# Two FFNs, an output projection and a pooling mixer joined into one stage over two token halves

## The chip, the cores and the metric

One of the eight cores of a Trainium2 chip runs the whole program. The metric is the device time of one execution in microseconds, the median of several executions. Besides the kernel there is nothing on the chip.

## What is computed

One inference step of a two-layer hybrid decoder, in fp32: 1024 prompt tokens and 8 sequences of 8 sample tokens, 1088 tokens of width 1024. Layer 0 mixes tokens by multi-head latent attention, layer 1 by causal mean pooling over windows of 2, 4, 8 and 16 tokens in four groups of 256 channels. Each mixer is followed by a gated FFN with a causal depthwise convolution of width 3. Around each sub-layer stand norms, with scale, shift and gate per sequence:

```python
xp = xp + g_mp[:, None, :] * rms_norm(op, norm_mix_post[i])
hp = modulate(xp, norm_ffn_pre[i], sh_fp, sc_fp)
...
u = h @ w_up                                   # 1024 -> 2 x 2816
up = jnp.concatenate([prev, u], axis=1)
conv = conv_b + up[:, 0:T] * conv_w[0]
for k in range(1, CONV_W):
    conv = conv + up[:, k:k + T] * conv_w[k]
y = (jax.nn.silu(conv[..., :D_FF]) * conv[..., D_FF:]) @ w_down
...
xp = xp + g_fp[:, None, :] * rms_norm(fp, norm_ffn_post[i])
```

Outputs are x of all tokens, the new attention cache rows, and the pooling and convolution states.

## The kernel before, in words

Channels lie on the partitions, tokens on the free axis; `k.x` holds x as 8 tiles of 128 channels by 1088 tokens. The tokens are cut into three chunks of 384, 384 and 320 columns (`CHUNKS`; the last has the 64 sample tokens). Precision comes from splitting each operand into a high part and a low part in fp32r, and each product is three matmuls: high by high, high by low, low by high. ScalarE makes the high part (`split_hi`, L1753), VectorE the low one (`split_lo`, L1814).

The stages follow one another, with a barrier between them (`stage_done`): `adaln_stage`, three attention stages, `mla_out_stage`, `ffn_stage(0)`, `pool_stage`, `ffn_stage(1)`.

- `mla_out_stage` multiplies the attention output by `wo` in 8 units of 128 rows (L1429 to L1431) and empties PSUM on ScalarE (L1390). Then comes `Exit`.
- `Exit` norms the result y: squares on ScalarE (L86), sums by a matmul with ones (L113), root (L95), turned to columns (L122), reciprocal on VectorE (L128), spread over the partitions (L143). VectorE multiplies y by gate and reciprocal (L519) and adds it to x (L524), half of the tiles on GpSimd (L532). It also takes the norm of the new x.
- `Entry` makes the next stage's input: x by scale and reciprocal (L418), shift and high part on ScalarE (L441), low part (L427, L431).
- `ffn_stage` runs over 22 pairs p: 128 gate channels G and 128 linear channels U each. Per pair SyncE fetches three units of 512 KB (L1720); TensorE forms G in three chunks of 8 x 3 matmuls, then U, and after each 3 matmuls of U one down product of the pair before (`down`, 3 matmuls into one of two banks, L1915 to L1917). ScalarE empties the banks (L1767, L1770), VectorE adds the other two taps (L1826, L1830), ScalarE does SiLU (L1794) and g's high part (L1789), VectorE the product (L1874) and g's low part (L1878). VectorE adds every down product to y in SBUF (`accumulate`, L1857), 24 per pair; `down` waits for `acc_done`, so that a bank is emptied before it is used again.
- `pool_stage` adds up window sums by doubling, two groups on VectorE (L1517, L1624) and two on GpSimd (L1517, L1556, L1557), those of the samples on VectorE (L1615, L1619), multiplies by four 256 x 256 matrices in plain fp32 (L1652, two passes each) and ends in `Exit`.

The order of the work on each engine is written out in the program: each engine has its own queue, in order, and semaphores tie them.

## Time and profile before

| | |
|---|---|
| median of 3 runs | 2976.69 us (2976.57 to 2980.84) |
| the profiled execution | 2976.89 us |
| its span, first to last instruction | 2975.1 us, 43092 instructions |
| mean granted clock of TensorE | 0.958 |
| TensorE busy | 2696.2 us (91%) |
| VectorE busy | 1772.6 us (60%) |
| ScalarE busy | 1028.8 us (35%) |
| GpSimd busy | 99.8 us (3%) |

The page cuts the span into 40 slices of 74 us, with the busy share in tenths (9 is 90% or more). The output projection begins at 959 us, FFN 0 at 1112, the pool mixer at 1970, FFN 1 at 2112. A granted clock of 1.00 is 2.4 GHz, 0.50 is 1.2 GHz.

### The profile page before, as it was taken

What the parts mean: (1) busy time and instruction counts of PE and PEld (TensorE: products, weight loads), DVE (VectorE), ACT (ScalarE), POOL (GpSimd) and SP (SyncE); (2) the same over time, 40 slices, a digit from 0 to 9 for tenths busy, and PEclk for the clock granted to TensorE, in tenths of its full rate; (3) what the DMA queues carried; (4) which work ended last, traced back from release to release, by engine and by line L of the source; (5) the groups of instructions that cost most, each with busy time, mean ns of one, the idle gap of its engine ahead of it and who ended that gap; (6) DMA issues with size and microseconds to landing.
All of it is one profiled execution on the core that took longest, in us unless ns stands there. A gap on an engine that the chain in (4) does not pass through costs nothing. (4 is left out here: it accounts for less than half of the span.)

```text
span 2975.1 us, 43092 instructions
## 1 busy us (share of the span) xinstructions
PE 2696.2 (91%) x15678; PEld 2321.5 (78%) x15678; DVE 1772.6 (60%) x3116; ACT 1028.8 (35%) x1692; POOL 99.8 (3%) x71
## 2 busy tenths in 40 slices
PE   6979699889978988999999999867799999999996
PEld 2558466666656958999999999723599999999993
DVE  3961355555623146666666666665666666666665
ACT  4842243434413144333333333233433333333322
POOL 0000000000000020000000000042100000000001
PEclk8989899999989999999999999988899999999998
DMA  7920100000063210111111111000111111111101
GB/s 295 413 75 32 48 12 22 11 25 0 1 209 107 103 36 29 43 43 51 50 47 42 42 42 42 13 29 0 43 47 51 50 43 42 42 42 42 42 28 66
DMA packets 42730, 178.48 MB, mean 60 GB/s; under 512 B 6146, under 2 KB 9730, under 8 KB 38690
## 3 DMA queue, kind: packets, MB, share of 16 engines
q1 hardware_dynamic: 41938, 176.81, 16.5%
q8 instruction: 45, 0.74, 0.1%
q10 hardware_dynamic: 720, 0.71, 0.1%
q14 instruction: 27, 0.22, 0.0%
HBM read 170.43 MB, written 7.07 MB: 60 GB/s over the span
## 5 line engine op out<-in xcount | busy, mean ns | idle before, releaser
L1857 DVE TENSOR_TENSOR ffn_y<-psum,ffn_y 128x384 f32<-128x384 f32 (+1 forms) x1056 | 554.7, 534 | 495.7 <-PE psum L1917 495.1
L1915 PE MATMUL psum<-ffn_h_hi,ffn_w_hi 128*128 128x384 f32 (+1 forms) x2112 | 692.9, 328 | 18.3 <-DVE ffn_h_lo L431 18.3
L1916 PE MATMUL psum<-ffn_h_lo,ffn_w_hi 128*128 128x384 f32 (+1 forms) x2112 | 695.4, 329 | 0.0
L1917 PE MATMUL psum<-ffn_h_hi,ffn_w_lo 128*128 128x384 f32 (+1 forms) x2112 | 692.1, 328 | 0.0
L1915 PEld LDWEIGHTS psum<-ffn_h_hi,ffn_w_hi 128*128 128x128 f32 x2112 | 399.1, 189 | 19.0 <-DVE ffn_h_lo L431 18.9
L1917 PEld LDWEIGHTS psum<-ffn_h_hi,ffn_w_lo 128*128 128x128 f32 x2112 | 399.4, 189 | 0.0
L1916 PEld LDWEIGHTS psum<-ffn_h_lo,ffn_w_hi 128*128 128x128 f32 x2112 | 399.0, 189 | 0.0
L1915 PE MATMUL psum<-ffn_g_hi,ffn_w_hi 128*128 128x384 f32 (+1 forms) x1056 | 357.6, 339 | 19.5 <-DVE ffn_g_lo L1878 15.1
L1916 PE MATMUL psum<-ffn_g_lo,ffn_w_hi 128*128 128x384 f32 (+1 forms) x1056 | 346.8, 328 | 0.0
L1917 PE MATMUL psum<-ffn_g_hi,ffn_w_lo 128*128 128x384 f32 (+1 forms) x1056 | 346.5, 328 | 0.0
L1767 ACT ACTIVATE ffn_u<-psum 128x384 f32<-128x384 f32 (+1 forms) x264 | 119.7, 454 | 548.4 <-PE psum L1917 442.8
L1915 PEld LDWEIGHTS psum<-ffn_g_hi,ffn_w_hi 128*128 128x128 f32 x1056 | 199.2, 189 | 52.9 <-DVE ffn_y L1857 28.7
L1826 DVE SCALAR_TENSOR_TENSOR ffn_work<-ffn_u,ffn_taps,ffn_work 128x1024 f32<-128x1024 f32 x176 | 225.4, 1281 | 16.0 <-ACT ffn_work L1770 13.5
L1916 PEld LDWEIGHTS psum<-ffn_g_lo,ffn_w_hi 128*128 128x128 f32 x1056 | 199.6, 189 | 0.0
L1917 PEld LDWEIGHTS psum<-ffn_g_hi,ffn_w_lo 128*128 128x128 f32 x1056 | 199.4, 189 | 0.0
L1770 ACT ACTIVATE ffn_work<-psum,ffn_taps 128x384 f32<-128x384 f32 (+1 forms) x264 | 172.9, 655 | 0.0
L1794 ACT ACTIVATE ffn_work<-ffn_work 128x1088 f32<-128x1088 f32 x44 | 49.0, 1114 | 351.1 <-DVE ffn_work L1830 351.1
L1814 DVE TENSOR_TENSOR ffn_w_lo<-ffn_raw,ffn_w_hi 128x1024 fp32r<-128x1024 f32 x132 | 157.5, 1219 | 20.6 <-ACT ffn_w_hi L1753 20.3
L1753 ACT ACTIVATE ffn_w_hi<-ffn_raw 128x1024 fp32r<-128x1024 f32 x132 | 135.6, 1065 | 49.5 <-DMA ffn_raw<-in_ffn_w 47.3
L1076 PE MATMUL psum<-keys,q 128*128 128x512 f32 (+3 forms) x384 | 146.2, 490 | 2.1 <-ACT prob L907 1.3
L914 ACT ACTIVATE prob_t<-psum 128x512 f32<-128x512 f32 (+3 forms) x128 | 66.2, 517 | 215.0 <-PE psum L1092 214.5
L337 DVE TENSOR_TENSOR ada_w_lo<-ada_w,ada_w_hi 128x2048 fp32r<-128x2048 f32 x48 | 107.7, 2287 | 23.1 <-ACT ada_w_hi L271 22.8
(230 smaller groups left out, 3637.1 us busy)
## 6 DMA issues: line engine op xcount, KB each, us to landing
ffn_raw<-in_ffn_w SPq DMA_DIRECT2D x132, 512.0 KB, 5.1
ada_w<-in_ada_w SPq DMA_DIRECT2D x24, 2048.0 KB, 10.7
cache<-in_cache SPq DMA_DIRECT2D x64, 320.0 KB, 4.9
x<-in_x SPq DMA_DIRECT2D x2, 4352.0 KB, 17.8
pair_raw<-in_pair_w SPq DMA_DIRECT2D x8, 768.0 KB, 4.4
wo_raw<-in_wo SPq DMA_DIRECT2D x8, 512.0 KB, 4.0
proj_raw<-in_proj_w SPq DMA_DIRECT2D x7, 512.0 KB, 3.8
out_x_out<-x SPq DMA_DIRECT2D x2, 1536.0 KB, 6.0
```

The lines of the kernel that those rows point to most:

```text
L337: dve.tensor_tensor(w_lo[:, s % 2, cols], w[:, s, cols], w_hi[:, s % 2, cols], ALU.subtract)\
L914: act.activation(prob_t[s][:, 0:w], turn_bank[:, o:o + w], ACT.Copy).then_inc(turned_a, 1)
L1076: last = pe.matmul(out[:, o:e], q[s][:, hh, b * P:(b + 1) * P], keys[s][:, hh, o:e], start=True, stop=True)
L1753: act.activation(w_hi[s][:], raw[s][:], ACT.Copy).then_inc(hi_ready[s], 1)
L1767: act.activation(u[s][:, 2 + t0:2 + t0 + w], bank[:, 0:w], ACT.Copy)
L1770: act.activation(conv[s][:, t0:t0 + n_], bank[:, 0:n_], ACT.Identity, bias=bias, scale=tap2)\
L1814: dve.tensor_tensor(w_lo[s][:], raw[s][:], w_hi[s][:], ALU.subtract).then_inc(lo_ready[s], 1)
L1826: dve.scalar_tensor_tensor(cp, u[s][:, tap:tap + SEQ], taps[:, bass.ds(m, 1), tap], cp, ALU.mult, ALU.add).then_inc(conv_step[s], 1)
L1857: dve.tensor_tensor(dst, down_bank[i % 2][:, 0:n_], dst, ALU.add).then_inc(acc_done, 1)
L1915: pe.matmul(bank[:, a], w_hi[s][:, w], act_hi, start=first, stop=False)
L1916: pe.matmul(bank[:, a], w_hi[s][:, w], act_lo, start=False, stop=False)
L1917: return pe.matmul(bank[:, a], w_lo[s][:, w], act_hi, start=False, stop=last)
```

## The change

`mla_out_stage`, both `ffn_stage`s and `pool_stage` go, with `Exit` and `last_x_norm`; `tail_stage` takes their place. It is one stage without a barrier inside. The tokens are cut into two halves of 544 and each half into two quarters of T = 272 columns (`lc` 0 and 1); half 1 ends with the sample tokens. The projection is 16 units (8 per half), the FFNs are 88 units n: layer 0 half 0, layer 0 half 1, layer 1 half 0, layer 1 half 1, 22 pairs each. Each weight is fetched and split once per half.

A unit is 8 x 3 matmuls for each quarter of G, then as many for each quarter of U. The down products are those of two units taken together: 4 of the 8 tiles of y in one unit, 4 in the next, so 8 down products of 6 matmuls per unit, two units later. They are issued after every second group of 3 matmuls of U. The laid-out `w_down` is reordered on the host to match.

What `Exit`, `Entry` and the window sums did is now in six chains. Each belongs to a half and runs beside the products of the other half (its host): after the projection of half 0 beside that of half 1, and so on. A `Plan` gives each step a tick; a unit has four ticks, one ahead of each quarter of G and U. The sum of squares goes: ScalarE squares a tile, GpSimd adds it to the others, TensorE multiplies once by ones over all partitions, ScalarE takes the root, VectorE the reciprocal. GpSimd also takes the windows of two groups and all of the samples.

```diff
+T = NT // 4
+HALF = 2 * T
...
+BETWEEN = Plan(
+    [("y", IN_ORDER, [by_twos(4, 5, 8, 9), by_twos(6, 7, 10, 11)], (11, 13),
+      [by_twos(14, 15, 16, 17), by_twos(18, 19, 20, 21)]),
+     ("x", IN_ORDER, [by_twos(16, 17, 18, 19), by_twos(20, 21, 22, 23)], (21, 25), None),
+     ("y", BY_GROUP, [by_twos(42, 43, 46, 50), by_twos(44, 45, 47, 51)], (52, 54),
+      [by_twos(55, 56, 57, 58), by_twos(59, 60, 61, 62)]),
+     ("x", IN_ORDER, [by_twos(57, 58, 59, 60), by_twos(61, 62, 63, 64)], (62, 66), None)],
+    [("pool", [by_twos(24, 25, 26, 27), by_twos(28, 29, 30, 31)], 32),
+     ("ffn", [by_twos(65, 66, 67, 68), by_twos(69, 70, 71, 72)], 74)],
+    34, (39, 41, 44, 48))
...
+        for half, host, plan, gates, entries, by_pool in (
+                (0, -1, AFTER_OUT_A, [(0, mix)], [ffn_in(0)], []),
+                (1, 0, AFTER_OUT_B, [(0, mix)], [ffn_in(0)], even),
+                (0, 1, BETWEEN, [(0, ffn), (1, mix)], [(1, SCALE_MIX, SHIFT_MIX), ffn_in(1)], even),
+                (1, 2, BETWEEN, [(0, ffn), (1, mix)], [(1, SCALE_MIX, SHIFT_MIX), ffn_in(1)], even),
+                (0, 3, LAST_A, [(1, ffn)], [], even),
+                (1, 4, LAST_B, [(1, ffn)], [], even)):
```

The queue of VectorE for the units, and that of ScalarE:

```diff
+            for n in range(N_PAIRS):                      # VectorE
+                q, p = divmod(n, PAIRS)
+                chain = chains[q + 1]
+                downs = [KT * (n - 2) + i for i in range(KT)] if n >= 2 else []
+                split_lo(dve, U, n)
+                if n >= 2:
+                    split_lo(dve, D, n - 2)
+                if n:
+                    convolve(dve, U, n - 1, 1)
+                    multiply(dve, n - 1, 1)
+                    split_g(dve, n - 1, 1)
+                chain.dve(dve, 4 * p)
+                convolve(dve, G, n, 0)
+                chain.dve(dve, 4 * p + 1)
+                convolve(dve, G, n, 1)
+                if n + 1 < N_PAIRS:
+                    split_lo(dve, G, n + 1)
+                for r in downs[0:2]:
+                    accumulate(dve, r)
+                chain.dve(dve, 4 * p + 2)
+                for r in downs[2:4]:
+                    accumulate(dve, r)
+                convolve(dve, U, n, 0)
+                multiply(dve, n, 0)
+                for r in downs[4:5]:
+                    accumulate(dve, r)
+                split_g(dve, n, 0)
+                for r in downs[5:6]:
+                    accumulate(dve, r)
+                chain.dve(dve, 4 * p + 3)
+                for r in downs[6:8]:
+                    accumulate(dve, r)
...
+                split_hi(act, U, n)                       # ScalarE
+                if n >= 2:
+                    split_hi(act, D, n - 2)
+                if n:
+                    evacuate(act, U, n - 1, 1)
+                    put_g(act, n - 1, 1)
+                chain.act(act, 4 * p)
+                evacuate(act, G, n, 0)
+                silu(act, n, 0)
+                chain.act(act, 4 * p + 1)
+                evacuate(act, G, n, 1)
+                silu(act, n, 1)
+                if n + 1 < N_PAIRS:
+                    split_hi(act, G, n + 1)
+                chain.act(act, 4 * p + 2)
+                evacuate(act, U, n, 0)
+                put_g(act, n, 0)
+                chain.act(act, 4 * p + 3)
```

`convolve` is two taps (four with samples), the second waiting for the first. `evacuate` copies a quarter to `u` and writes the scaled copy to `conv`; with samples it also moves their rows and the states. TensorE's down product and its place:

```diff
+            def down(r):
+                m, lc, kt = down_tile(r)
...
+                pe.wait_ge(t.lo_ready, number[D, m] + 1)
+                pe.wait_ge(t.g_lo_ready, 2 * (first + 1) + lc + 1)
+                if r >= 2:
+                    pe.wait_ge(t.acc_done, r - 1)
+                for e in range(2):
...
+                    pe.matmul(bank, t.w_hi[i][:, o], hi, start=e == 0, stop=False)
+                    pe.matmul(bank, t.w_hi[i][:, o], lo, start=False, stop=False)
+                    last = pe.matmul(bank, t.w_lo[i][:, o], hi, start=False, stop=e == 1)
+                last.then_inc(t.down_done, 1)
...
+                    if s == U and n >= 2 and kt % 2:
+                        down(KT * (n - 2) + 4 * lc + kt // 2)
...
+            for n in range(N_PAIRS):
+                q, p = divmod(n, PAIRS)
+                chain = chains[q + 1]
+                for i, (s, lc) in enumerate(((G, 0), (G, 1), (U, 0), (U, 1))):
+                    chain.pe(pe, 4 * p + i)
+                    up(s, n, lc)
```

SyncE fetches the weight units into two buffers, each fetch waiting for the low part of the unit two before (`lo_ready`); x, the pool weights and states, and the outputs are moved between these fetches:

```diff
+            def load(o):
+                if o >= 2:
+                    sp.wait_ge(t.lo_ready, o - 1)
+                sp.dma_start(t.raw[o % 2][:], unit(*order[o])).then_inc(t.raw_in[o % 2], 16)
```

## Rows read from the trace of the kernel before

**Rows 1.** The page's slices of the span, TensorE.

```profile
PE   6979699889978988999999999867799999999996
```

**Rows 2.** Busy time of each engine by stretch, granted clock, DMA share, GB/s.

```profile
1058.80:1112.00 53.20, 42.88 (x169) 16.60 (x168) 31.65 (x64) 26.63 (x35) 20.12 (x13) 0.97 0.11 40
...
1168.00:1860.00 692.00, 690.63 (x4140) 679.77 (x4139) 472.27 (x829) 214.44 (x364) 0.00 (x0) 1.00 0.13 43
...
1937.20:2112.00 174.80, 120.72 (x417) 53.54 (x416) 110.23 (x143) 65.89 (x87) 66.51 (x38) 0.84 0.07 24
```

**Rows 3.** Timeline of TensorE: start us, us, instruction, [idle before and what ended it].

```profile
1049.67 0.33 PE L1430 MATMUL psum<-o_lo,wo_hi 128*128 128x384 f32 x1
...
1055.22 0.31 PE L1429 MATMUL psum<-o_hi,wo_hi 128*128 128x320 f32 x1
...
1058.58 0.31 PE L1431 MATMUL psum<-o_hi,wo_lo 128*128 128x320 f32 x1
...
1131.32 0.63 PE L1915 MATMUL psum<-ffn_h_hi,ffn_w_hi 128*128 128x320 f32 x1 [9.15 <-DVE ffn_h_lo L431]
...
1914.47 0.66 PE L1915 MATMUL psum<-ffn_g_hi,ffn_w_hi 128*128 128x384 f32 x1 [7.55 <-DVE ffn_g_lo L1878]
...
2029.48 24.33 PE L1652 MATMUL psum<-pooled,pool_w 128*128 128x384 f32 x72 [6.50 <-DVE pooled L1624]
...
2939.33 0.82 PE L122 MATMUL psum<-ones,ffn_work 1*128 1x1 f32 x6
```

**Rows 4.** Groups of instructions by shape, TensorE: busy us, mean ns.

```profile
L1060 PE MATMUL psum<-pair_raw,ckv 128*128 128x128 f32 x256 | 31.9, 278 | 3.7 <-ACT keys L896 3.7
```

**Rows 5.** Groups of instructions by shape, VectorE.

```profile
L1857 DVE TENSOR_TENSOR ffn_y<-psum,ffn_y 128x320 f32<-128x320 f32 x352 | 172.7, 492 | 131.0 <-PE psum L1917 131.0
...
L524 DVE TENSOR_TENSOR x<-x,ffn_y 128x256 f32<-128x256 f32 x8 | 3.4, 424 | 0.1
...
L1826 DVE SCALAR_TENSOR_TENSOR ffn_work<-ffn_u,ffn_taps,ffn_work 128x1024 f32<-128x1024 f32 x176 | 225.4, 1281 | 16.0 <-ACT ffn_work L1770 13.5
...
L1830 DVE SCALAR_TENSOR_TENSOR ffn_work<-ffn_u,ffn_taps,ffn_work 128x64 f32<-128x64 f32 x176 | 49.1, 279 | 0.0
...
L1814 DVE TENSOR_TENSOR ffn_w_lo<-ffn_raw,ffn_w_hi 128x1024 fp32r<-128x1024 f32 x132 | 157.5, 1219 | 20.6 <-ACT ffn_w_hi L1753 20.3
```

**Rows 6.** Groups of instructions by shape, ScalarE.

```profile
L1753 ACT ACTIVATE ffn_w_hi<-ffn_raw 128x1024 fp32r<-128x1024 f32 x132 | 135.6, 1065 | 49.5 <-DMA ffn_raw<-in_ffn_w 47.3 <-DVE ffn_h_lo L431 2.2
...
L1770 ACT ACTIVATE ffn_work<-psum,ffn_taps 128x320 f32<-128x320 f32 x88 | 54.9, 623 | 0.0
...
L1767 ACT ACTIVATE ffn_u<-psum 128x256 f32<-128x256 f32 x88 | 33.9, 386 | 321.2 <-PE psum L1917 321.2
...
L1794 ACT ACTIVATE ffn_work<-ffn_work 128x1088 f32<-128x1088 f32 x44 | 49.0, 1114 | 351.1 <-DVE ffn_work L1830 351.1
...
L95 ACT ACT_TABLE_LOAD x4 | 5.1, 1283 | 0.1
```

**Rows 7.** Timeline of VectorE and ScalarE in FFN 1.

```profile
2238.53 1.02 DVE L1857 TENSOR_TENSOR ffn_y<-psum,ffn_y 128x384 f32<-128x384 f32 x2
...
2913.43 1.11 ACT L1805 ACTIVATE ffn_g_hi<-ffn_work 128x1088 fp32r<-128x1088 f32 x1 [3.47 <-DVE ffn_work L1874]
...
2914.57 1.29 DVE L1878 TENSOR_TENSOR ffn_g_lo<-ffn_work,ffn_g_hi 128x1088 fp32r<-128x1088 f32 x1
```

**Rows 8.** Timeline of VectorE and GpSimd in the pool mixer.

```profile
2003.82 3.62 DVE L1619 SCALAR_TENSOR_TENSOR pooled<-pool_sum_s,pool_hs 128x128 f32<-128x128 f32 x1
...
2002.85 4.44 POOL L1517 TENSOR_TENSOR pool_sum_p<-pool_h 128x2076 f32<-128x2076 f32 x1
```

**Rows 9.** Timeline of TensorE in the attention stage.

```profile
469.49 2.34 PE L1107 MATMUL psum<-prob_t,vals 128*64 128x128 f32 x28 [1.99 <-DVE prob_t L989]
```

**Rows 10.** Busy time by stretch, just behind that pause.

```profile
470.50:473.90 3.40, 3.40 (x24) 3.03 (x20) 0.38 (x2) 0.06 (x1) 0.00 (x0) 0.50 0.02 5
```

**Rows 11.** DMA issues: KB each, us to landing.

```profile
ffn_raw<-in_ffn_w SPq DMA_DIRECT2D x132, 512.0 KB, 5.1
```

More of the change, by code:

```diff
@@ L1458, in mla @@
         k.stage_done()
-        mla_out_stage(k, m)
-        k.stage_done()
 WINDOWS = (2, 4, 8, 16)
@@ L1469, with width, by_twos, by_fours @@
 SW = BUF + DEC_S
-def pool_stage(k):
+T = NT // 4
+HALF = 2 * T
+SAMPLE_AT = HALF - NS
+N_PAIRS = 4 * PAIRS
+TICKS = 4 * PAIRS
+OUT_UNITS = 2 * KT
+G, U, D = range(3)
+POOL_ORDER = (0, 2, 1, 3)
+POOL_BY_POOL = (0, 1)
+IN_ORDER = list(range(KT))
+BY_GROUP = [g * GT + mo for g in POOL_ORDER for mo in range(GT)]
+def width(half, lc):
+    return T - NS if half and lc else T
+def by_twos(*ticks):
+    return [t for tick in ticks for t in (tick, tick)]
+def by_fours(*ticks):
+    return [t for tick in ticks for t in (tick,) * 4]
@@ new lines, in tail_stage, with slot, unit @@
+        order = [("out", j) for j in range(OUT_UNITS)] + [(G, 0)]
+        for n in range(N_PAIRS):
+            order += [(U, n)] + ([(D, n - 2)] if n >= 2 else []) + ([(G, n + 1)] if n + 1 < N_PAIRS else [])
+        order += [(D, N_PAIRS - 2), (D, N_PAIRS - 1)]
+        number = {what: o for o, what in enumerate(order)}
+        def slot(s, n):
+            if s == "out":
+                return (n + 1) % 3
+            return G if s == D and n == N_PAIRS - 2 else s
+        def unit(s, n):
+            if s == "out":
+                return io["wo"][n % KT]
+            return io["ffn_w"][n // PAIRS // 2, n % PAIRS, s]
@@ L1966, in program @@
+            for tick in range(6):
+                chains[5].pe(pe, tick)
 def program(nc, io):
```

1406 lines of the change are left out of this document (806 added, 600 removed).

## The prediction

> **What bounds the kernel now.** I read the page's slices first: TensorE's row is at 9 for most of the span and drops three times, near 40%, between 65% and 70%, and at the end [rows 1]. The busy times by stretch say what the drops are: the FFN loop keeps TensorE busy for 690.6 of 692 us at full clock, while the stretch from the end of the output projection to the first FFN product is 53.2 us, the one from the last product of FFN 0 over the pool mixer to FFN 1 174.8 us [rows 2]. The timeline of TensorE gives the smaller holes: 9.15 us in front of the third chunk of the first pair and 7.55 us in front of the last down-projection [rows 3], each once in each FFN. So the kernel is bound by products inside the FFNs and by norms, residuals and pool sums between them.
>
> **What is removed.** 53.2 + 174.8 + 2 x 9.15 + 2 x 7.55 + 35.9 (from the end of the last product, 2939.2 [rows 3], to 2975.1) = 297 us. Half-clock starts and the 24 last down products, which wait for their sums, cost some 16 us more in each FFN (22.7 us where their 72 products need 11.8). Total 329, floor 2975 - 329 = 2646. To this comes back what must be done anyway: the pool products (72 of 96 take 24.3 us [rows 3]; all in quarters some 31), 28 sums of squares at 0.5 us (two passes, from the same row's 0.34 us for 384 columns) = 14, and an exit for the last half of 23 us (last squares and POOL sums 3, root with its table 1.8, two quarters of gating 12, copy out 6). **2714 us** if nothing else changes.
>
> **TensorE's own work.** Products shrink from 384 or 320 columns to 272, with the same total of columns. Between 1049.67 and 1055.22 32 products of 384 columns start every 0.1734 us, and after that 23 of 320 every 0.146 [rows 3]; the line through both gives 0.125 for 272. Four such are 0.500 for 1088 columns, three of before 0.493, which takes a gain of 22 us of loop overhead back. A bound above: with 128 columns in two-cycle passes a product with its weight load takes 31.9/256 = 0.125 [rows 4], so the weights don't bind at 272; 0.137 (8% more, as if the overhead grew) is the upper end. The rule of the Trainium skill (TensorE: Matmul & The Clock Gate, "Wait — 56ns, not 53.3ns?") is a fixed 2.5 ns on top of the columns, 0.116 here; the trace's 384-column spacing is 11 ns above what it gives, so the measurement decides; by the page the sum would be some 50 us lower.
>
> **The new order inside a unit.** The FFNs become 88 units (22 pairs x 2 halves x 2 layers), each 96 up and 48 down products = 144 x 0.125 = 18.0 us. A down product of 6 matmuls goes to one of two banks, and the third has to wait until VectorE has added the first. In its queue (the loop over `n` in the vector block) the first `accumulate` stands behind: `split_lo` of U and D, `convolve` and `multiply` of U's second quarter of the unit before, its `split_g`, `convolve` of both quarters of G, and `split_lo` of the next G. These wait in turn for ScalarE. Prices at 272 columns from the rows on either side: add or product 0.44, tap 0.50 (1.28 at 1024, 0.28 at 64 columns), low part of a weight 1.22 [rows 5]; ScalarE copy from PSUM 0.40, scaled copy 0.59, SiLU or g's high part 0.44, weight's high part 1.06 [rows 6]. An instruction right behind another starts 0.08 before the first one's end; a hand-over between engines costs 0.03 [rows 7]. From the last product of the unit before (0): drain 0.25, last add 0.36, U and D low 2 x 1.14 = 2.89; taps 2 x 0.53, product 0.44 = 4.39; g high 4.86; ScalarE empties G's first quarter, 5.67; taps 6.73; SiLU 7.20; second quarter 8.0; taps 9.07; SiLU and next G's high part 10.52; its low part 11.69; first add 12.13. TensorE stands there after 78 products = 9.75 us. It pauses 2.45 us (the row that shows the method right is the end of FFN 1, where the same kind of walk over taps, product, high and low part gives the 7.55 us hole of [rows 3]), then does its other 66 products: period 12.2 + 8.25 = **20.45 against 18.0**. In the half with the sample tokens small copies and taps (0.1 to 0.2 each, as the 64-column tap) add 0.75: 21.2. The first two units have no down products, so 42 x 2.45 + 44 x 3.2 = 244 us. Of the 45 us of TensorE's sums and pool products some 35 fall into these pauses. 2714 + 244 - 35 = **2923**.
>
> **The norms put beside the products.** Their steps sit at four places (ticks) of a unit; those at the first two lie on the path above, because VectorE and ScalarE, not TensorE, set the pace there. For one of the two long chains: squares 6 x 0.7 = 4; square roots 2 on the path, 1.28 of table load each [rows 6] plus root, and small waits for the SiLU table after the others, 5; gating 8 x 0.8 = 6; new inputs 8 x 1.5 = 12; window sums on VectorE 3; pool outputs 3; one pool product 2. Total 35, two chains 70; the chain after the projection 16, the two last 10. **Some 100 us.** Bounds: 0 if all hides in waits, 200 if every tick counts.
>
> **GpSimd beside VectorE.** At 2003.82 a VectorE operation on 128 columns with two SBUF inputs took 3.62 us, where a tap on 64 takes 0.28 [rows 5], and ended with GpSimd's operation of 2002.85 [rows 8]. The new stage gives GpSimd window sums of some 16 us in one half, 32 with the samples, and 44 short adds per long chain; VectorE's taps, splits and products, all with two SBUF inputs, stand on the path. I take 37 for the windows and 18 for the short adds: **55 us**, ends 0 and 130. The Trainium skill (SBUF — State Buffer, "SBUF: two separate sides") says that GpSimd and VectorE take this port exclusively for a whole instruction and the other one blocks; the row agrees. By that rule each short add counts too, and the sum would go to the upper end.
>
> **The clock.** After a pause of 1.99 us [rows 9] TensorE's granted clock was 0.50, the 1.2 GHz level, for 3.4 us [rows 10]. The pauses here are 2.45 and 3.2 us, longer with a chain; but a pause may fall so that nothing follows, as most short pauses of that stage. Each 3.4 us at half clock loses 1.7. I count 35 of 86 as half clocks, **60 us**; ends 0 and 150.
>
> **Loads.** Each weight is fetched and split once per token half: 264 fetches for 132, 8.5 us of ScalarE and VectorE per pair more, counted above. With two buffers the next G's fetch goes out at 1.75 and lands 5.1 us later [rows 11], ahead of 9.5: nothing, at the other end a wait of 1 us per unit. The queue of SyncE carries x, the states and the pool weights between the fetches; each waits for something long done and costs one issue (0.3 to 0.7), inside that slack. GpSimd runs its chain steps in order too, and TensorE waits for its last add before each sum; it is due a tick or more later, so nothing, with the windows as the exception (rivals). The down adds halve in number, but they weren't on the path.
>
> **Sum:** 2923 + 100 + 55 + 60 = 3138, with the 1.8 us between this execution's span and its time **3140 us**. That execution's 2976.9 us stands 0.2 above the median of 2976.7. A measurement of this kernel tells 0.2%, 6 us.
>
> **Rivals.** *TensorE stays the bound* (the other side): if the path to the first add is under 9.75 us, the pause is gone and with it the clock term: 2714 to 2900, decided at 2.4 us of path. For it speaks only that VectorE works 11 us of 18 (3 low parts 3.4, 8 taps 3.4, 4 products and low parts 1.4, 8 adds 2.9); against it that each of the waits is in the code in order. 0.12. *The pause is there but the norms hide in it*: 2925 to 2965; the forecast turns into a gain when chains, port and clock together cost under 50 us. For it: half of the ticks lie where there are 1.5 us of slack. 0.08. *Port and clock at their upper ends*: above 3290; for it rows 8, 9, 10; it needs blocking by all the short adds or a half clock in nearly every unit. 0.10. *The halves don't overlap at all*, since TensorE's in-order queue waits for each chain's sums or its pool inputs: the sample windows, 18 small operations on GpSimd, are due 31 us after their start; 10 to 40 us more, inside the range. 0.04 in the part above 3250. The rest, 0.66, is the forecast, 2990 to 3290; 0.03 falls within 0.2% of before.
>
> **Range.** 2900 to 3290: leaves out most of the first rival and of the third. Faster 0.20, the same 0.03, slower 0.77.
>
> **What would show it.** Right: TensorE idle some 2.5 us in front of the third down product in every unit, released by VectorE's add; units of 20 to 22 us in quiet stretches; VectorE's operations during GpSimd's windows several times longer; half-clock stretches all through the FFNs; no hole over 10 us. Wrong: units of 18 us, or pauses elsewhere (weights, evacuation), or a drop of PE's product rate at 272 columns to 0.137.

## The result, and the profile after

The changed kernel takes 3282.5 us (median of 4 runs, 3280.5 to 3283.9) against 2976.6 us (median of 4 runs, 2974.6 to 2980.8) for the kernel before: a ratio of 1.103, 95% interval 1.102 to 1.105. It is slower by 306 us. The forecast was 3140 us with a range up to 3290: the sign and the range held, the point was 142 us too low.

The page of the changed kernel, the parts that answer to [rows 1]: its span, the busy times, TensorE's row of slices and the granted clock.

```profile
span 3282.1 us, 49338 instructions
...
PE 2706.9 (82%) x18538; PEld 2441.6 (74%) x18538; DVE 1896.5 (58%) x3561; ACT 1354.6 (41%) x3004; POOL 269.6 (8%) x293
...
PE   6977889889789878988877787888778788888885
...
PEclk9988999999899889999888898999889899998888
```

The three deep drops of [rows 1] are gone, as the change means them to be. In their place every slice behind the first third loses a little, and the clock's row, which was at 9 in the FFNs, has an 8 in every second or third place. The mean clock of the execution is 0.915, against 0.958 before.

What TensorE waited for behind 1060 us (engine, line, operand and its releaser; us in total, times, the longest):

```profile
PE psum L2295 <- DVE t_y L2196: 284.1, 77, 14.9
PE psum L1870 <- ACT t_y L1647: 40.7, 9, 5.7
PE psum L2295 <- DVE t_y L2194: 26.7, 7, 8.2
PE psum L1855 <- ACT t_stat L1593: 19.0, 6, 3.8
PE psum L1855 <- POOL t_stat L1785: 12.3, 6, 5.0
PE psum L1870 <- DVE t_rooms L1744: 3.5, 1, 3.5
```

L2295 is the first product of a down tile, L2196 and L2194 are VectorE's sum and its first copy: 310.8 of 390 us (two groups of under 2 us each aren't shown) are the wait that the prediction put there, 84 times over the 86 units. The rest is the pool products (L1870) and the sums of squares (L1855), which wait for ScalarE and GpSimd.

The same wait in TensorE's timeline (start, duration, instruction; in brackets the idle time before it and its releaser). First units of the half without samples, then units of the half with them, then one in which GpSimd is at its window sums, and a pool product:

```profile
1356.25 0.57 PE L2295 MATMUL psum<-t_g_hi,t_w_hi 128*128 128x272 f32 x1 [2.25 <-DVE t_y L2196]
1378.31 0.36 PE L2295 MATMUL psum<-t_g_hi,t_w_hi 128*128 128x272 f32 x1 [2.26 <-DVE t_y L2196]
1398.88 0.36 PE L2295 MATMUL psum<-t_g_hi,t_w_hi 128*128 128x272 f32 x1 [2.26 <-DVE t_y L2196]
...
2900.31 0.37 PE L2295 MATMUL psum<-t_g_hi,t_w_hi 128*128 128x272 f32 x1 [2.85 <-DVE t_y L2196]
2921.48 0.36 PE L2295 MATMUL psum<-t_g_hi,t_w_hi 128*128 128x272 f32 x1 [2.85 <-DVE t_y L2196]
...
2944.17 0.57 PE L2295 MATMUL psum<-t_g_hi,t_w_hi 128*128 128x272 f32 x1 [2.84 <-DVE t_y L2196]
2968.03 0.56 PE L2295 MATMUL psum<-t_g_hi,t_w_hi 128*128 128x272 f32 x1 [2.84 <-DVE t_y L2196]
...
1759.68 0.56 PE L2295 MATMUL psum<-t_g_hi,t_w_hi 128*128 128x272 f32 x1 [14.88 <-DVE t_y L2196]
...
1826.65 3.96 PE L1870 MATMUL psum<-t_y,t_rooms 128*128 128x272 f32 x8 [5.72 <-ACT t_y L1647]
```

One pause in each unit, 2.26 us in one half and 2.85 in the other. Where the clock stays full behind it, the distance to the next pause is 20.57 us and 21.17 us. Where a half clock follows, it is 22.06 us (from 1356.25) and 22.7 us (from 2921.48). From 2944 us on the pause is the same 2.84 us, but the distance is 23.9 us. The first product shows the lower clock: it takes 0.57 us and not 0.36. Of the 17 units with a pause of 2.26 us 6 have a half clock in them, of the 19 with one of 2.85 us 17, and of the other 50, with norm steps and longer or several pauses, 48.

The windows of time (start and end, length, then the busy us and instructions of TensorE, its weight loads, VectorE, ScalarE and GpSimd, then the granted clock, the DMA share and GB/s) show it directly, in the 3.4 us behind one such pause, in the next two stretches of the same length, and as the mean over a quiet stretch of either half:

```profile
2968.00:2971.40 3.40, 3.37 (x15) 3.40 (x16) 0.68 (x2) 0.27 (x3) 0.00 (x0) 0.50 0.48 154
2971.40:2974.80 3.40, 3.40 (x19) 3.40 (x19) 1.82 (x5) 1.20 (x4) 0.00 (x0) 0.60 0.00 0
2974.80:2978.20 3.40, 3.40 (x29) 3.40 (x28) 1.62 (x4) 0.02 (x1) 0.00 (x0) 1.00 0.02 5
1271.00:1546.00 275.00, 245.63 (x1873) 243.17 (x1874) 161.59 (x300) 103.19 (x221) 0.00 (x0) 0.97 0.24 75
2944.17:3206.91 262.74, 231.34 (x1584) 229.22 (x1585) 140.22 (x298) 94.58 (x275) 0.00 (x0) 0.86 0.21 67
```

Why the sum is late is seen in VectorE's timeline of one quiet unit with samples, with ScalarE's part of the step that comes just before (two answers):

```profile
2909.27 2.36 DVE L2147 TENSOR_TENSOR t_w_lo<-t_raw,t_w_hi 128x1024 fp32r<-128x1024 f32 x2
...
2914.64 1.04 DVE L2164 SCALAR_TENSOR_TENSOR t_conv<-t_u,t_taps,t_conv 128x272 f32<-128x272 f32 x2 [0.51 <-ACT t_conv L2069]
2917.14 0.43 DVE L2164 SCALAR_TENSOR_TENSOR t_conv<-t_u,t_taps,t_conv 128x208 f32<-128x208 f32 x1 [1.45 <-ACT t_conv L2069]
...
2919.75 1.23 DVE L2147 TENSOR_TENSOR t_w_lo<-t_raw,t_w_hi 128x1024 fp32r<-128x1024 f32 x1 [1.44 <-ACT t_w_hi L2038]
2920.90 0.78 DVE L2196 TENSOR_TENSOR t_y<-psum,t_y 128x272 f32<-128x272 f32 x2
```

```profile
2918.34 0.43 ACT L2075 ACTIVATE t_conv<-t_conv 128x272 f32<-128x272 f32 x1 [1.24 <-DVE t_conv L2169]
2918.68 1.04 ACT L2038 ACTIVATE t_w_hi<-t_raw 128x1024 fp32r<-128x1024 f32 x1
```

Low parts of U and D, G's taps after two waits for ScalarE, then 1.44 us of waiting for the high part of the next G and its low part, and only then, at 2920.90, the first two sums; the third down product starts at 2921.48. VectorE is idle for some 4 us of these 12: the order of its queue makes the pause, not the amount of its work.

The last reading is in the window phase, VectorE's and GpSimd's timelines (two answers):

```profile
1749.57 2.54 DVE L2164 SCALAR_TENSOR_TENSOR t_conv<-t_u,t_taps,t_conv 128x208 f32<-128x208 f32 x1 [1.73 <-ACT t_conv L2069]
1752.04 2.14 DVE L2169 SCALAR_TENSOR_TENSOR t_conv<-t_u,t_taps,t_conv 128x64 f32<-128x64 f32 x1
1754.10 0.42 DVE L2164 SCALAR_TENSOR_TENSOR t_conv<-t_u,t_taps,t_conv 128x208 f32<-128x208 f32 x1
1754.44 2.06 DVE L2169 SCALAR_TENSOR_TENSOR t_conv<-t_u,t_taps,t_conv 128x64 f32<-128x64 f32 x1
```

```profile
1749.47 2.41 POOL L1824 TENSOR_TENSOR t_y<-t_rooms,t_y 128x1058 f32<-128x1058 f32 x1
1752.05 2.04 POOL L1744 TENSOR_TENSOR t_rooms<-t_y 128x1116 f32<-128x1116 f32 x1 [0.17 <-POOL t_y L1824]
```

A tap on 64 columns, 0.28 us elsewhere, takes 2.14 while GpSimd's operation takes 2.04 beside it: it ends when GpSimd's does. The third row, which starts before GpSimd's next operation, runs in the 0.42 us that it takes anyway; the fourth is held up again.

### The profile page after: what moved, and what is told of

Read it like the earlier page. It is cut to its first block, busy times and chain, and to the rows that moved or that the text cites. A ratio compares the mean times of both kernels' runs of the same rounds, so it can differ in the third digit from the quotient of the medians.

```text
span 3282.1 us, 49338 instructions
## 1 busy us (share of the span) xinstructions
PE 2706.9 (82%) x18538; PEld 2441.6 (74%) x18538; DVE 1896.5 (58%) x3561; ACT 1354.6 (41%) x3004; POOL 269.6 (8%) x293
## 4 chain that ended last, share of the span: by engine, by line
PE 31%; DVE 24%; ACT 10%; issue 4%; POOL 0%; ACTq 0%; DMA 0%; DVEq 0%; POOLq 0%
DVE t_w_lo L2147 9%; DVE t_conv L2164 7%; PE psum L2295 5%; PE psum L2296 5%; PE psum L2297 5%; PE psum L2319 4%; PE psum L2317 4%; PE psum L2318 4%; ACT t_w_hi L2038 3%; ACT t_conv L2069 2%; DVE t_y L2196 2%; ACT t_u L2060 1%; PE psum L1870 1%; DVE t_conv L2169 1%; DVE t_conv L2176 1%
## 5 line engine op out<-in xcount | busy, mean ns | idle before, releaser
L2317 PE MATMUL psum<-t_h,t_w_hi 128*128 128x272 f32 x2816 | 848.0, 301 | 0.0
L2319 PE MATMUL psum<-t_h,t_w_lo 128*128 128x272 f32 x2816 | 841.4, 299 | 0.0
L2318 PE MATMUL psum<-t_h,t_w_hi 128*128 128x272 f32 x2816 | 837.5, 297 | 0.0
L2295 PE MATMUL psum<-t_g_hi,t_w_hi 128*128 128x272 f32 x1408 | 446.1, 317 | 312.4 <-DVE t_y L2196 284.1
L2317 PEld LDWEIGHTS psum<-t_h,t_w_hi 128*128 128x128 f32 x2816 | 559.6, 199 | 2.5
L2318 PEld LDWEIGHTS psum<-t_h,t_w_hi 128*128 128x128 f32 x2816 | 559.3, 199 | 2.3
L2319 PEld LDWEIGHTS psum<-t_h,t_w_lo 128*128 128x128 f32 x2816 | 558.3, 198 | 0.0
L2295 PEld LDWEIGHTS psum<-t_g_hi,t_w_hi 128*128 128x128 f32 x1408 | 295.6, 210 | 329.0 <-DVE t_w_lo L2147 325.9
L2196 DVE TENSOR_TENSOR t_y<-psum,t_y 128x272 f32<-128x272 f32 x640 | 273.8, 438 | 387.6 <-PE psum L2297 387.2
L2164 DVE SCALAR_TENSOR_TENSOR t_conv<-t_u,t_taps,t_conv 128x272 f32<-128x272 f32 x704 | 357.0, 507 | 243.6 <-ACT t_conv L2069 234.0
L2147 DVE TENSOR_TENSOR t_w_lo<-t_raw,t_w_hi 128x1024 fp32r<-128x1024 f32 x280 | 336.5, 1228 | 175.0 <-ACT t_w_hi L2038 175.0
L2296 PE MATMUL psum<-t_g_lo,t_w_hi 128*128 128x272 f32 x1408 | 434.5, 309 | 0.0
L2297 PE MATMUL psum<-t_g_hi,t_w_lo 128*128 128x272 f32 x1408 | 431.3, 306 | 0.0
L2296 PEld LDWEIGHTS psum<-t_g_lo,t_w_hi 128*128 128x128 f32 x1408 | 297.1, 211 | 0.0
## 6 DMA issues: line engine op xcount, KB each, us to landing
x<-in_x SPq DMA_DIRECT2D x1, 4352.0 KB, 22.7
```

The source lines that it names most:

```text
L2147: dve.tensor_tensor(t.w_lo[i][:], t.raw[o % 2][:], t.w_hi[i][:], ALU.subtract).then_inc(t.lo_ready, 1)
L2164: dve.scalar_tensor_tensor(prompt, u[:, lc * T + tap:lc * T + tap + w], by, prompt, ALU.mult, ALU.add)\
L2196: dve.tensor_tensor(y, t.down_bank[r % 2][:, 0:T], y, ALU.add).then_inc(t.acc_done, 1)
L2295: pe.matmul(bank, t.w_hi[i][:, o], hi, start=e == 0, stop=False)
L2296: pe.matmul(bank, t.w_hi[i][:, o], lo, start=False, stop=False)
L2297: last = pe.matmul(bank, t.w_lo[i][:, o], hi, start=False, stop=e == 1)
```

## The experiments

Twelve kernels ran. All ratios below are to the kernel before, timed on the same chip; differences in us are between medians. Not all kernels ran on the same chip, and the kernel before took 2973.0 to 2977.3 us on the different ones, so that a difference in us between two of them can be off by up to 4 us.

**The first two sums ahead of the next G's low part.** This takes one step away from what stands before the sums, and changes nothing else.

```diff
                 convolve(dve, G, n, 1)
+                for r in downs[0:2]:
+                    accumulate(dve, r)
                 if n + 1 < N_PAIRS:
                     split_lo(dve, G, n + 1)
-                for r in downs[0:2]:
-                    accumulate(dve, r)
```

> Edit: in VectorE's queue the first two sums of down products go ahead of the low part of the next G weight. Queue theory: the pause of 2.26 us (half A) and 2.85 us (half B) in front of the third down product exists because these adds stand behind that low part, 1.2 us, and behind the wait for its high part; with them ahead it goes to 0 to 0.3 us in quiet units, the period from 20.57 and 21.17 us to 18.1 to 18.6, and the half clocks that follow the pauses go with it: 86 x 2.4 = 206 us of pauses and some 120 us of clock, to 2920 to 3000 us. Rival (the whole walk of VectorE and ScalarE sets the pace, and the pause only shows where the slack lies): the period stays above 20 us, the pause comes back in front of another product, 3200 us or more.

3016.8 us, ratio 1.014 (1.012 to 1.015): 266 us less than the changed kernel, 17 us above the range that the queue theory gave and far from the rival's. Its largest wait, two pauses of its last quiet stretch, and that stretch's window:

```profile
PE psum L2295 <- DVE t_y L2196: 116.5, 62, 13.0
```

```profile
2720.56 0.36 PE L2295 MATMUL psum<-t_g_hi,t_w_hi 128*128 128x272 f32 x1 [0.18 <-DVE t_y L2196]
2739.06 0.36 PE L2295 MATMUL psum<-t_g_hi,t_w_hi 128*128 128x272 f32 x1 [0.18 <-DVE t_y L2196]
```

```profile
2665.12:2960.88 295.76, 292.85 (x2304) 289.77 (x2305) 202.43 (x433) 137.62 (x400) 0.00 (x0) 1.00 0.29 94
```

The pause is 0.18 us, the unit 18.50 us, the clock 1.00. In the half without samples the quiet units have no pause at all and take 18.03 to 18.11 us. The rival, that the whole walk of VectorE and ScalarE sets the pace, is out for the quiet units. The waits for the sums fell by 183 us (with L2194: 310.8 to 127.7), the time by 266. The rest is the clock's part and that of the stops: TensorE's busy time, for the same products, fell by 80 us, from 2706.9 to 2626.7. The pool products' wait is untouched (40.7 us).

**One sum further ahead.** The first sum goes between G's two convolutions, outside the units of the pool products.

```diff
+                busy = any(at - 1 <= 4 * p + 3 and at + 2 >= 4 * p for at in chain.plan.products)
+                early = 0 if busy else 1
+                for r in downs[0:early]:
+                    accumulate(dve, r)
                 convolve(dve, G, n, 1)
+                for r in downs[early:2]:
+                    accumulate(dve, r)
                 if n + 1 < N_PAIRS:
                     split_lo(dve, G, n + 1)
-                for r in downs[0:2]:
-                    accumulate(dve, r)
```

> Edit: as the run before, and the very first sum of down products goes still further ahead, between the two convolutions of G (outside the units of the pool products). Queue theory: the first sum is then never late, another 0 to 0.3 us per unit in half B and up to 1 us in units where the norms put work between the convolutions: 2880 to 2980 us. Rival (VectorE now waits for TensorE at that place and so delays the rest of its queue): slower than the run before by 0 to 60 us. If the pace is set elsewhere: 3200 us or more.

3018.6 us, ratio 1.014 (1.012 to 1.016): no different from the run before (3016.8), and a miss of the forecast. TensorE's waits for the sums were 126.2 us instead of 127.7. Outside the units of the pool products, what was left of the pauses isn't the first sum's place; once the low part of G was out of the way, moving it on bought nothing.

**The pause filled with products.** Nothing is moved. TensorE does 20 products that nobody reads in the place where it would be idle.

```diff
+                if r % KT == 2 and r < KT * (N_PAIRS - 2):
+                    ...
+                        for _ in range(20):
+                            pe.matmul(k.banks[7][:, 0:240], t.w_hi[i][:, 0:P], t.h[:, q % 2, 0, 0, 0:240],
+                                      start=True, stop=True)
                 if r >= 2:
                     pe.wait_ge(t.acc_done, r - 1)
```

> Edit: nothing is moved; in front of the third down product TensorE does 20 extra products of 240 columns (2.3 us) into a bank that nobody reads, outside the units around the pool products. That fills the pause and leaves its end where it is. If the half clock behind the pauses costs what I read from the trace (2.7 us per unit in the last eleven units, 1.5 us in part of the others; 436 us at half clock, half of it lost, at least part of it behind these pauses): 3110 to 3200 us, the last stretch of half B at 21.2 us per unit and not 23.9, and a mean clock above 0.94. Rival (the lost time at half clock would be spent in the pause anyway, since VectorE sets the pace): 3260 to 3300 us with the clock up. If my estimate of the extra products is too long for quiet units, each loses 0.2 us, 15 us in all.

3210.3 us, ratio 1.079 (1.077 to 1.080): 72 us less by doing more work, 10 us above the theory's range and 50 below the rival's; the mean clock was 0.945, as forecast. Two units of the last stretch, and its window:

```profile
2878.05 0.39 PE L2301 MATMUL psum<-t_g_hi,t_w_hi 128*128 128x272 f32 x1 [0.53 <-DVE t_y L2196]
2899.16 0.39 PE L2301 MATMUL psum<-t_g_hi,t_w_hi 128*128 128x272 f32 x1 [0.52 <-DVE t_y L2196]
```

```profile
2880.00:3110.00 230.00, 224.25 (x1791) 222.15 (x1789) 139.37 (x296) 94.50 (x275) 0.00 (x0) 1.00 0.22 75
```

The unit takes 21.1 us, as the walk of VectorE and ScalarE gives, with the clock at 1.00; without the extra products it took 23.9 at 0.86. So the half clock is a cost of its own and not time that would be waited for anyway, and some 72 us is a lower bound of it: the longer pauses of the units with norm steps weren't filled whole (12.6 us was still the longest).

**GpSimd's windows cut short.** On the changed kernel GpSimd's window sums work on 48 columns, and on one sample sequence; most of its window sums are left out.

```diff
         h = t.y[:, self.half, g * GT:(g + 1) * GT, 0:W]
+        W = 48
         n = doublings(g)
```

> Edit: GpSimd's window sums work on the first 48 columns of 287 and on one of the sample sequences, so most of its window sums are left out; everything else is as in the changed kernel. Port theory (VectorE's operations with two SBUF inputs stand still for the length of GpSimd's operation): the holes of 14.88 us and 10.72 us in front of down products fall to 5 to 8 us, operations such as the 64-column tap go from 2.1 us back to 0.3, and the two window phases save 25 to 60 us: 3225 to 3260 us. Rival (the window phases are long because of their own number of steps): 3275 to 3290 us, the holes stay.

3264.6 us, ratio 1.097 (1.095 to 1.099): 18 us less, between the two forecasts: more than the rival's, under the 25 to 60 of the port theory. In the same unit the tap on 64 columns is back at 0.28 us (VectorE), and the hole of 14.88 us became 7.58 (TensorE; two answers):

```profile
1742.30 0.28 DVE L2170 SCALAR_TENSOR_TENSOR t_conv<-t_u,t_taps,t_conv 128x64 f32<-128x64 f32 x1
```

```profile
1746.28 0.56 PE L2296 MATMUL psum<-t_g_hi,t_w_hi 128*128 128x272 f32 x1 [7.58 <-DVE t_y L2197]
```

The mechanism is there, since the same tap with a short GpSimd operation beside it isn't held up, and its price is smaller than I thought.

**No reciprocals.** On the changed kernel the 28 reciprocals are copies, so the division by the norms is left out.

```diff
-            dve.reciprocal(self.stat(n, lc), self.stat(n, lc)).then_inc(t.inverted, 1)
+            dve.tensor_copy(self.stat(n, lc), self.stat(n, lc)).then_inc(t.inverted, 1)
```

> Edit on the changed kernel itself: the 28 reciprocals of 272 columns are plain copies, so the division by the norms is left out. A reciprocal takes 1.85 us where a copy takes 0.44: 39 us of VectorE go. Theory (VectorE's queue is the path, and I never priced the reciprocals): those at the first two ticks of a unit count, and some half clocks behind long pauses go: 15 to 40 us less, 3242 to 3267 us. Rival (they lie in VectorE's slack): 3278 to 3285 us.

3255.9 us, ratio 1.095 (1.092 to 1.097): 27 us less, in the theory's range. The group in the changed kernel (behind 1060 us) that I had left out of the sum:

```profile
L1657 DVE RECIPROCAL t_stat<-t_stat 128x272 f32<-128x272 f32 x24 | 44.3, 1845 | 2.5 <-ACT t_stat L1593 2.5
```

**VectorE's norm steps cut short.** Reciprocals, gatings and adds to x on 16 columns; most of that work is left out.

```diff
-            dve.reciprocal(self.stat(n, lc), self.stat(n, lc)).then_inc(t.inverted, 1)
+            dve.reciprocal(self.stat(n, lc)[:, 0:16], self.stat(n, lc)[:, 0:16]).then_inc(t.inverted, 1)
...
+            y = y[:, 0:16]
...
-        dve.tensor_tensor(x, x, t.y_tile(self.half, lc, kt), ALU.add).then_inc(t.x_by_dve, 1)
+        dve.tensor_tensor(x[:, 0:16], x[:, 0:16], t.y_tile(self.half, lc, kt)[:, 0:16], ALU.add).then_inc(t.x_by_dve, 1)
```

> Edit on the changed kernel itself: VectorE's reciprocals (28), its gatings (128) and its adds to x (72) of the norms work on 16 columns instead of 272, so most of that work is left out; some 128 us of VectorE's time go (28 x 1.67, 128 x 0.44, 72 x 0.35). Theory (in the units with norm steps the first sum stands behind them in VectorE's queue, about half of them at the two ticks ahead of it): 50 to 90 us less with the clock, 3190 to 3235 us; 27 of that is the reciprocals, by the run without them. Rival (most of it lies where VectorE waits anyway): 3240 to 3256 us.

3244.8 us, ratio 1.091 (1.089 to 1.093): 38 us less where I expected 50 to 90; the rival was right. VectorE's busy time fell by 97 us (1896.5 to 1799.3; I had estimated 128), the time by 38, of which 27 are the reciprocals. The waits for the sums only went from 310.8 to 288.0 us. Most of VectorE's norm work lies where VectorE waits.

**Pool products two ticks apart.** The next six kernels stand on the one with the first two sums ahead (3016.8 us), each on the one before it; the last two both stand on the one at 2945.9 us. Here the squares, sums, gates and inputs behind the pool products are 3 to 4 ticks later too.

```diff
-            if at <= tick < at + 2:
-                yield 2 * i + tick - at, POOL_ORDER[i], tick - at
+            if tick in (at, at + 2):
+                lc = (tick - at) // 2
+                yield 2 * i + lc, POOL_ORDER[i], lc
...
-    34, (39, 41, 44, 48))
+    34, (39, 43, 47, 51))
...
-    [("y", IN_ORDER, [by_twos(4, 5, 8, 9), by_twos(6, 7, 10, 11)], (11, 13),
+    [("y", IN_ORDER, [by_twos(4, 5, 8, 9), by_twos(6, 7, 10, 11)], (11, 14),
```

> Edit on top of the run with the first two sums ahead (3016.8 us): the two token quarters of a pool product are two ticks apart instead of one, the first squares, sums, gates and inputs behind them 3 to 4 ticks later, and the second sum of each norm 3 ticks behind the first instead of 2. Theory (TensorE waits 44 us for ScalarE to empty the pool banks and 11 us for ScalarE's root, because those stand behind an evacuation and a g high part in ScalarE's queue within the same tick): these waits go, a part of it comes back in front of down products: 2965 to 2990 us. Rival (these waits only use time that VectorE needs anyway in those units): 3005 to 3020 us.

2974.6 us, ratio 1.000 (0.999 to 1.001): 42 us less, by the time what the theory said, by the waits only half: those for ScalarE's root fell from 19.0 to 4.7 us, those of the pool products from 44.2 to 30.7, those for the sums rose by 6.5, and the mean clock went from 0.946 to 0.950, worth 12 us. A row of its waits, and one of ScalarE's timeline (two answers):

```profile
PE psum L1873 <- ACT t_y L1648: 30.7, 8, 12.1
```

```profile
2256.64 1.06 ACT L2041 ACTIVATE t_w_hi<-t_raw 128x1024 fp32r<-128x1024 f32 x1 [13.00 <-DMA t_raw<-in_ffn_w]
```

The pool products still waited, some 2.6 or 2.7 us in seven cases and 12.1 once. In the short waits the emptying stands behind g's high part, for which ScalarE waits 2.1 us for VectorE's product. The long one isn't GpSimd's, which had done its last sample window at 2203 us, and not the squares', as I took it when I planned the pool ticks below: ScalarE waits 13.00 us for a weight. That fetch had been issued right behind the pool states' output at 2225.5 us, 480 KB in packets of under 512 B, 29.9 us from issue to landing, for most of which the DMA engines are some nine tenths busy at 14 to 57 GB/s. That the output holds the fetch up is what the times suggest; no run moves it. Neither the changed kernel nor the one with the sums ahead has a ScalarE wait for a weight in this part; all six from here on have one of 10 to 16 us.

**Down products later in the unit.** VectorE's third to eighth sums are spread to match.

```diff
-                    if s == U and n >= 2 and kt % 2:
-                        down(KT * (n - 2) + 4 * lc + kt // 2)
+                    if s == U and n >= 2 and (lc, kt) in DOWN_AT:
+                        down(KT * (n - 2) + DOWN_AT.index((lc, kt)))
...
+DOWN_AT = ((0, 5), (0, 7), (1, 1), (1, 2), (1, 3), (1, 5), (1, 6), (1, 7))
```

> Edit on top of the run before: TensorE does the first down product behind the 6th tile of U's first quarter (was the 2nd) and the third behind the 2nd tile of U's second quarter, so that it needs the first sum 1.5 us later in the unit; VectorE's sums 2 to 7 are spread to match. Queue theory: each pause of the units with norm steps, 3 to 5 us in about 30 of them, is shorter by up to 1.5 us, the half clocks behind some go too: 35 to 60 us less than the run before, 2915 to 2950 us. Rival (the later products of a unit now wait in their turn, since 6 sums stand in its last 6.8 us): no gain or a loss of up to 80 us, with pauses at the 5th to 8th product.

2970.4 us, ratio 0.999 (0.998 to 1.000): 4 us, a miss. The longest pauses got shorter (12.2 to 9.6 us), but there are 105 waits for the sums instead of 74, with the total 123.4 us instead of 134.2: the rival, in which the later products of a unit wait in their turn.

**Adds to x on VectorE.**

```diff
-                (0, 1, BETWEEN, [(0, ffn), (1, mix)], [(1, SCALE_MIX, SHIFT_MIX), ffn_in(1)], even),
+                (0, 1, BETWEEN, [(0, ffn), (1, mix)], [(1, SCALE_MIX, SHIFT_MIX), ffn_in(1)], []),
...
```

> Edit on top of the run before: GpSimd's 88 short adds of gated outputs to x are done by VectorE (0.44 us each, 39 us of its time, in two thirds of the units with norms on the path). Port theory as I priced it (each short add holds a VectorE operation up for up to its own 0.9 us): 0 to 40 us saved. Rival (short adds rarely meet an operation with two SBUF inputs, and VectorE's own time counts): 15 to 35 us slower than the run before.

2968.6 us, ratio 0.998 (0.997 to 0.999), 2 us from the run before, inside the scatter. The groups of VectorE's gatings and adds show why it is neutral. With GpSimd doing half of the adds:

```profile
L1706 DVE SCALAR_TENSOR_TENSOR t_y<-t_y,ada,t_stat 128x272 f32<-128x272 f32 (+1 forms) x128 | 82.1, 655 | 0.1
...
L1733 DVE TENSOR_TENSOR x<-x,t_y 128x272 f32<-128x272 f32 (+1 forms) x72 | 39.1, 546 | 0.5
```

and with VectorE doing all (the 56 of GpSimd too, not 88 as I had put in the expectation):

```profile
L1706 DVE SCALAR_TENSOR_TENSOR t_y<-t_y,ada,t_stat 128x272 f32<-128x272 f32 (+1 forms) x128 | 69.9, 556 | 0.1
...
L1733 DVE TENSOR_TENSOR x<-x,t_y 128x272 f32<-128x272 f32 (+1 forms) x128 | 57.1, 456 | 0.0
```

56 more adds cost VectorE 18.0 us, and the gatings take 12.2 us less. GpSimd's help with 46 us of adds relieves VectorE of 6 us: two thirds of what it takes over come back in slower gatings.

**Pool products where ScalarE has emptied the bank.** Each quarter's tick is written out and the steps behind follow; the chain ends at tick 82 instead of 78, and the first chain's sum of x is one tick later.

```diff
-    34, (39, 43, 47, 51))
+    34, ((39, 42), (44, 47), (50, 52), (55, 58)))
```

> Edit on top of the run with x's adds on VectorE (2968.6 us): each quarter of a pool product has its tick written out, so that ScalarE's emptying of the bank before it lies a whole ScalarE step ahead of TensorE; the squares behind it follow, the last tick of the long chain goes from 78 to 82 of 88; the first chain's sum of x is one tick later. Theory (TensorE waits 2.6 us eight times and 11.5 us once for ScalarE, the long one because ScalarE's squares wait for GpSimd, which is still at the sample windows): 31 us of waits go, 5 to 10 of them return elsewhere, and the 5 us in front of the first chain's sum go: 2935 to 2955 us. Rival (those units are paced by VectorE anyway): 2960 to 2970 us.

2945.9 us, ratio 0.990 (0.989 to 0.992): 23 us less, as expected. Of the pool products' waits 0.6 us is left, but the long one only moved: ScalarE now waits 15.3 us for the weight behind the states' output, and TensorE 7.3 us for that weight's low part. The waits for the sums are 128 us (122 in the run before), and the hole of the window phase is still there (waits, then timeline):

```profile
PE psum L2299 <- DVE t_y L2200: 115.9, 83, 9.6
PE psum L2299 <- DVE t_y L2198: 12.0, 17, 3.8
...
PE psum L2321 <- DVE t_w_lo L2151: 7.3, 1, 7.3
...
PE psum L1874 <- ACT t_y L1649: 0.6, 1, 0.6
```

```profile
1672.96 0.57 PE L2299 MATMUL psum<-t_g_hi,t_w_hi 128*128 128x272 f32 x1 [9.59 <-DVE t_y L2200]
```

**The second tick's norm steps moved behind G's second convolution.**

```diff
-                chain.dve(dve, 4 * p + 1)
                 convolve(dve, G, n, 1)
                 for r in downs[0:1]:
                     accumulate(dve, r)
+                chain.dve(dve, 4 * p + 1)
...
-                chain.act(act, 4 * p + 1)
                 evacuate(act, G, n, 1)
+                chain.act(act, 4 * p + 1)
```

> Edit on top of the run before: in each unit the norm steps of the second tick stand behind G's second convolution (VectorE: behind the first sum too; ScalarE: behind G's second evacuation) instead of ahead of it. Theory (in units with norm steps the first sum is late because these steps, 0.9 to 1.8 us, stand ahead of it): another 20 to 45 us less than the run before. Rival (in those units VectorE and ScalarE have more than a unit's worth of work, so the steps only delay something later): within 10 us of the run before.

2963.1 us, ratio 0.996 (0.995 to 0.998): 17 us slower than the run before, where neither forecast had it more than 10 us slower. TensorE's waits for the sums are nearly the same (130.7 us against 127.9), but its mean clock is 0.946 against 0.957, which over 2950 us is 32 us of full speed, and its busy time for the same products is 14 us longer (2622.8 against 2608.6). The same amount of waiting fell so that more half clocks followed; why these, stays open.

**GpSimd's windows in halves.** On the 2945.9 us kernel each of the prompt windows' operations is two of half the size.

```diff
-            self.add_window(pool, g, step, sums).then_inc(t.window_p, 1)
+            for j in range(GT):
+                last = self.add_window(pool, g, step, sums, j)
+            last.then_inc(t.window_p, 1)
```

> Edit on top of the run at 2945.9 us: GpSimd's window sums over the prompt columns are issued as two operations of one tile each instead of one of two tiles, the same work in pieces half as long. Port theory (a VectorE operation with two SBUF inputs stands still until the GpSimd operation in progress is over, 2.1 to 2.5 us now): held up operations take 1.1 to 1.4 us, the hole of 9.59 us in front of a down product falls to 5 to 7, 3 to 12 us less: 2934 to 2943 us. Rival (GpSimd's next operation takes the port again at once, so the total held up is the same): within 3 us of 2946.

2943.4 us, ratio 0.990 (0.988 to 0.991). The hole of 9.59 us is two pauses of 3.04 and 2.59 now:

```profile
1664.06 0.36 PE L2306 MATMUL psum<-t_g_hi,t_w_hi 128*128 128x272 f32 x1 [3.04 <-DVE t_y L2207]
...
1670.19 0.57 PE L2306 MATMUL psum<-t_g_hi,t_w_hi 128*128 128x272 f32 x1 [2.59 <-DVE t_y L2207]
```

but the time moved by 2.5 us only, inside the rival's forecast and just above the theory's, and all waits for the sums together only from 127.9 to 126.2 us. The time decides nothing between the two, though the trace shows the hole shrink as the port theory says. This kernel beats both: 31 us (1.0%) under the kernel before, 339 us under the changed one, with the same work.

## Why the prediction was right in sign and range, and 142 us short

By its own terms, against the changed kernel's span of 3282.1 us (forecast 3138):

- **The pause and where it comes from: right.** Forecast 2.45 and 3.2 us, periods of 20.45 and 21.2; measured 2.26 and 2.85, 20.57 and 21.17 at full clock. The first two sums ahead of G's low part took it away. That the two periods are right with shorter pauses means that the base of 18.0 was short: a unit is 18.31 us without its pause (20.57 - 2.26), where units that don't stop at all take 18.03 to 18.11. Products start every 0.125 us as forecast (the fixed 2.5 ns of the Trainium skill, "TensorE: Matmul & The Clock Gate", section "Wait — 56ns, not 53.3ns?", would have given 0.116: the trace disagrees). The upper end of 0.137 is 10% above it and not 8%; it played no part. The other 0.3 us is what a stop costs beside its wait: the row of the last product before it goes on 0.17 us beyond where the next one would have started, and the first one after it takes 0.36 us instead of 0.29, 0.24 of the 0.3. 86 units x 0.31 = 27 us that weren't in the sum.
- **TensorE's waits: nearly right in sum, from other parts.** Forecast 244 - 35 + 100 + 55 = 364 us, measured 390. But VectorE's norm work on the path is 38 us, 27 of it reciprocals that I had not listed at all; the windows cost 18 and the short adds next to nothing in the time, where I had 55 for both. What I had not put in a place of its own: 44 us in which pool products wait for the banks to be emptied and window sums, and 31 for roots and GpSimd's sums of squares. The prediction had 5 us of small waits for them and put GpSimd's last adds at "nothing", being due a tick or more later; they come at other places of the unit than the pause and add to it. The runs with the spaced ticks took 42 and 23 us out. The sign "no hole over 10 us" failed too: the window phases have one of 14.88 and one of 10.72 us.
- **The clock: the term that failed.** I took 35 half clocks of 1.7 us, 60 us, with 150 as the upper end. By the mean clocks the changed kernel loses (1 - 0.915) x 3282 = 279 us of full speed and the one before (1 - 0.958) x 2975 = 125: 154 more. These means count idle time too. Counted only where TensorE is busy, the half clocks behind 1060 us lose 161 us, in the kernel before 29. Filling the pauses with products gave 72 us back at least. The first count of the estimate, the share of units with a half clock, was right only for the pauses of 2.26 us (6 of 17, where the prediction took 35 of 86); over all units it was 71 of 86. The second, its price, was right for a single one (22.06 - 20.57 = 1.5 us, forecast 1.7) and low for the last eleven periods (0.50 for 3.4 us and 0.60 for 3.4 more, 2.7 us lost in each). I had a range for it and took a value below its middle because in [rows 10] one pause of 1.99 us had it and most short ones of that stage didn't; the pauses here were longer and regular, so that the upper end was the nearer row.
- **The port: right as a mechanism, too large as a price.** VectorE's operations with two SBUF inputs end with GpSimd's, as [rows 8] had shown, and with GpSimd's operations cut short they are back at 0.28 us. The Trainium skill (SBUF — State Buffer, "SBUF: two separate sides") says that whichever of the two starts first holds their shared port pair for the whole instruction and the other is blocked; the rows at 1752 us agree. The windows cost 18 us where I took 37. By the counts of the trace a long chain has 64 short adds on GpSimd (48 for the sums of squares, 16 to x) and not 44.
- **Loads: right for this kernel.** A weight's low part is in only one of TensorE's waits behind the projection, of 1.7 us, and ScalarE never waits for a fetch there. In the faster kernels it does, once, as said above.

27 us for the stops, 26 for the waits and 101 (161 - 60) for the clock make 154 us where 144 were missing; the 10 us too many are in terms that no run takes apart. The range held by 8 us only, and not because its terms did: the clock was at its upper end and beyond, while the port was far under its own. The rival with port and clock at their upper ends was half right: the clock was there and the port wasn't. The rival that TensorE stays the bound is what the quiet units do once the sums stand ahead of G's low part.

What stays open: 126 us of waits for the sums are left even in the fastest kernel. Short VectorE steps and short windows were tried on the changed kernel only, where they took 23 and 13 us off the 311; ScalarE's steps (squares, inputs, table loads) weren't taken out by themselves, nor was the pool states' output.

## What to carry to other kernels

When two pieces of work are interleaved in queues that run in order, ask for each short instruction that releases the bound engine what stands ahead of it and what that waits for: here two sums of 0.4 us stood behind a 1.2 us step whose result TensorE needed only some 8 us later (66 products of 0.125 us), and their place decided 266 us. A pause that comes once in every period costs its length, 0.3 us for stopping, and often a half clock behind it: here in a third of the units at 2.26 us and in nine of ten at 2.85 us. An idle engine's time isn't all worth the same: taking 97 us of VectorE's work out was worth 38, changing the order of two instructions seven times that. And when the largest wait is gone, read again what ended each of the rest, on the engine that was waited for too: the 12 us wait "for ScalarE" was a wait for a weight.

## What the runs showed of the hardware that was not expected

- The same pause of 2.85 us was followed by full clock (21.17 us per unit), by one stretch at half clock (22.7 us), and, from 2944 us on, by a longer one in each of eleven periods (23.89 us). The runs don't tell what tips it from one to the other.
- After a pause in that last rhythm the clock stayed low for more than 3.4 us: 0.50, then 0.60 in the next 3.4 us, then 1.00.
- Twenty useless products in a pause make a kernel 72 us faster.
- Two orders of the norm steps with equal waits (127.9 and 130.7 us) differ by 0.011 in mean clock and 17 us in time.
- While 480 KB went out in packets of under 512 B, a 512 KB weight fetch issued right behind took so long that ScalarE waited 13.0 us for it; its other waits for fetches there are 0.2 us at most.
- GpSimd's adds beside VectorE: 56 adds taken from GpSimd cost VectorE 18.0 us more and give 12.2 us back in its other operations.
